# RWKV-7 chunks: Z and Y formed transposed in one product per head, and Y turned back before its norm

## The chip, the cores and the metric

One Trainium2 chip, one core. The time is the device time of one execution in microseconds (us), median of three runs. "Profile" is the hardware profiler's record of one execution.

## The reference, cut to what matters

A decoder layer for 1040 prompt rows (16 meta tokens, 1024 prompt rows) and 8 sample rows. One branch of it is RWKV-7 time mixing with 8 heads of 64 channels. Its recurrence, run over the prompt rows one by one:

```python
def step(state, inp):
    r_t, w_t, k_t, v_t, kk_t, a_t = inp
    s_kk = jnp.einsum('bhvk,bhk->bhv', state, kk_t)
    state = (state * w_t[:, :, None, :]
             - s_kk[..., None] * (kk_t * a_t)[:, :, None, :]
             + v_t[..., None] * k_t[:, :, None, :])
    return state, jnp.einsum('bhvk,bhk->bhv', state, r_t)
...
mu = jnp.mean(y, axis=-1, keepdims=True)
var = jnp.mean(jnp.square(y - mu), axis=-1, keepdims=True)
y = ((y - mu) * lax.rsqrt(var + GN_EPS)).reshape(bsz, t, D_RWKV)
y = y * lw['ln_x_w'].astype(f32) + lw['ln_x_b'].astype(f32)
out = (y + bonus.reshape(bsz, t, D_RWKV)) * g
```

The rest of the layer (forgetting attention, gates, output projection, MLP) is not touched by the change.

## The kernel before, in words

The prompt is cut into NC = 10 chunks of C = 104 rows. Each chunk replaces the loop over rows by products of 104 rows at once, for 8 heads (h), which lie as 4 pairs (p) of two halves (e) of 64 partitions. Engines run their own instruction streams and meet through counted steps: `ch_pe`, `ch_act`, `ch_dve`, `ch_pool`, with `wait(...)` on a named step. A chunk goes like this.

1. Prologue. DVE: four scans (L1891), lm (L1893), r (L1895), k (L1897), b (L1898), a (L1900), with three exponentials on ACT between them. DVE and ACT start it when PE has turned back Y of the chunk before (step "yt", `y_back`, L995).
2. PE turns K, B, V to natural layout (`natural`, L1006, 12 transposes), then forms the products of K and B with AR (L1053, 208 columns moving). DVE masks them into MK and MB (L1909).
3. Z, in natural layout (rows of the chunk on partitions): MK standing, V moving (L1062), and AR standing, the state St moving (L1065). ACT copies it to Zm.
4. DVE prepares the start of a triangular inverse (L1916, L1918, L1922) and subtracts a weight tile for the filler (L589); then six levels of halving: PE t1 (L1022, L1023), ACT copies, PE t2x, DVE subtracts (L1939). Levels 1 to 4 use these forms, 5 and 6 smaller ones (L1090, L1103, L1112).
5. u = inverse by Z (L1129); ACT negates it to NU. Y in natural layout: AR by St (L1133), MK by V (L1136), then MB by NU (L1141). Then the state's product (L1145, L1148), "s".
6. DVE: sum and mean of Y per head, state_sum and state (L1976, L1978), center, sq, var; ACT Ln and Exp; DVE norm (L1984). PE turns Y back (`y_back`), ACT scales it (L1595), POOL adds the bonus and multiplies by the gate (L2335, L2338).

Between these steps PE works on another job, the input projection of the attention branch and the gates: `fill.run(n)` issues n pieces of 3 matmuls (L384, L385, L386), 48 pieces in each chunk. Where they stand, and how many, is written by hand. Each piece is independent of the chunk's own data. The first chunk's pieces are one full-precision matmul each (L388). Between chunk 0 and 1 DVE makes eight low halves of the filler's input (L1990); the first eight pieces of chunk 1 wait for one each.

After the last chunk PE, DVE and SP start the sample rows; SP loads the samples' state dS when the chunk steps of PE and DVE are done.

Of the kernel before, what the change touches and what calls it, by code (L numbers as in the profile page):

```python
# [39 lines left out]
AX = mybir.AxisListType  # L40

P = 128
# [7 lines left out]
C = 104  # L50
NC = TP // C
HD = 64
NH = 8
# [78 lines left out]
def build(nc, A):  # L132
    with ExitStack() as ctx:
# [416 lines left out]
        NU = T1.rearrange("p a b -> p (a b)")  # L550
        Yc = Xm.rearrange("p a b -> p (a b)")
# [42 lines left out]
        LEVELS = range(1, N_LV)  # L594
# [3 lines left out]
                      + [f"{t}_{lv}_{q}" for lv in LEVELS for t in ("t1", *(("t2x",) if lv < N_LV - 1 else ()),  # L598
                                                                    *(("t2",) if lv >= N_LV - 2 else ()))
                         for q in range(2)]  # L600
                      + ["u", "y", "s", "yt"])
        ch_act = Steps(sem("ch_act"), ["v", "e1", "e3", "e2", "nat_k", "z"]
                       + [f"t1_{lv}_{q}" for lv in LEVELS for q in range(2)]
                       + ["nu", "ln", "rstd"] + [f"y_{p}" for p in range(HP)])
# [6 lines left out]
                       + ["sum", "mean", "state_sum", "state", "center", "sq", "var", "norm"])  # L611
# [41 lines left out]
        def _(sp):  # L653
# [116 lines left out]
            sp.dma_start(A["o_sp"], St).then_inc(sp_stored, 16)  # L770
            sp.dma_start(dS.rearrange("p b h k -> p (b h k)"), A["st"]).then_inc(ds_load, 16)
# [120 lines left out]
        def _(pe):  # L892
# [105 lines left out]
            def pe_chunk(c):  # L998
# [29 lines left out]
                def z_out(e, p):  # L1028
                    return PS[0:C, 2 + e, p * HD:(p + 1) * HD]
# [40 lines left out]
                for lv in LEVELS[:-1]:  # L1070
                    for q in range(2):
                        if q == 0:
                            pe.wait_ge(ch_pool.sem, ch_pool.after(c, f"bm_{lv}_low"))
                        if lv > 1:
                            wait(ch_dve, f"x_{lv - 1}_{q}_x")
                        for j in range(4):
                            last = by_halves(q, j, Bm[lv % 2], Xm, 4 * q + j)
                        ch_pe.done(last, f"t1_{lv}_{q}")
                    if IN_LEVEL[lv - 1]:
                        fill.run(IN_LEVEL[lv - 1])  # L1080
                    for q in range(2):
                        wait(ch_act, f"t1_{lv}_{q}")
                        if lv > 1:
                            wait(ch_dve, f"x_{lv - 1}_{q}_xt")
                        for j in range(4):
                            h = 4 * q + j
                            if lv < N_LV - 2:
                                last = by_halves(2 + q, j, XTr, T1, h)
                            else:
                                last = pe.matmul(PS[top, 2 + q, j * HB:(j + 1) * HB], XTr[top, h], T1[top, h],  # L1090
                                                 start=True, stop=True)
                        ch_pe.done(last, f"t2x_{lv}_{q}")
                for q in range(2):
                    for j in range(4):
                        last = by_halves(4 + q, j, T1, XTr, 4 * q + j)
                    ch_pe.done(last, f"t2_{N_LV - 2}_{q}")

                lv = N_LV - 1
                for q in range(2):
                    wait(ch_dve, f"x_{lv - 1}_{q}_x")  # L1100
                    for j in range(4):
                        h = 4 * q + j
                        last = pe.matmul(PS[low, q, j * HB:(j + 1) * HB], MB[top, h, 0, low], Xm[top, h],  # L1103
                                         start=True, stop=True)
                    ch_pe.done(last, f"t1_{lv}_{q}")
                fill.run(2)
                for q in range(2):
                    wait(ch_act, f"t1_{lv}_{q}")
                    wait(ch_dve, f"x_{lv - 1}_{q}_xl")
                    for j in range(4):  # L1110
                        h = 4 * q + j
                        last = pe.matmul(PS[top, 4 + q, j * HB:j * HB + HR], T1[low, h], XTF[low, h, low],  # L1112
                                         start=True, stop=True)
                    ch_pe.done(last, f"t2_{lv}_{q}")
# [4 lines left out]
                def y_out(e, p):  # L1119
                    return PS[0:C, 2 + e, p * HD:(p + 1) * HD]  # L1120

# [3 lines left out]
                fill.run(2)  # L1125
                wait(ch_act, "z")
                wait(ch_dve, f"x_{N_LV - 1}_1_xt")
                for h, e, p, rows in by_rows():
                    last = pe.matmul(u_out(e, p), XTF[0:C, h], Zm[0:C, h * HD:(h + 1) * HD], start=(p == 0),  # L1129
                                     stop=(p == HP - 1), skip_group_check=True)  # L1130
# [19 lines left out]
                ch_pe.done(last, "s")  # L1150
                fill.run()
# [299 lines left out]
        def _(act):  # L1451
# [77 lines left out]
            def act_chunk(c, gates, early=True):  # L1529
# [12 lines left out]
                act.wait_ge(ch_dve.sem, ch_dve.before(c))  # L1542
                act.wait_ge(st_in, 16 * c + 16)
# [13 lines left out]
                ch_act.done(act.copy(Zm[0:C].rearrange("p (e n) -> p e n", e=2), PS[0:C, 2:4, 0:HP * HD]), "z")  # L1557
# [5 lines left out]
                for lv in LEVELS:  # L1563
                    for q in range(2):
# [3 lines left out]
                        part = slice(0, C) if lv < N_LV - 1 else low  # L1568
                        ch_act.done(act.copy(quad(T1, q)[part], PS[part, q, 0:4 * HB]), f"t1_{lv}_{q}")
# [13 lines left out]

                wait(ch_dve, "var")
# [195 lines left out]
        def _(dve):  # L1780
# [99 lines left out]
            def dve_chunk(c, early=True):  # L1880
# [50 lines left out]
                for lv in LEVELS:  # L1931
# [3 lines left out]
                    if lv < N_LV - 1:  # L1935
                        part = slice(0, C) if lv < N_LV - 2 else top
                        for q in range(2):
                            wait(ch_pe, f"t2x_{lv}_{q}")
                            done(dve.tensor_tensor(quad(Xm, q)[part], quad(Xm, q)[part], PS[part, 2 + q, 0:4 * HB],  # L1939
                                                   ALU.subtract), f"x_{lv}_{q}_x")  # L1940
                    for q in range(2):
# [5 lines left out]
                        if lv < N_LV - 1:  # L1947
                            done(dve.tensor_tensor(XTF[top, four, top], XTr[top, four], moved(4 + q, top, HB),
                                                   ALU.subtract), f"x_{lv}_{q}_xt")
                            done(dve.tensor_tensor(XTF[low, four, low], XTr[low, four, 0:HR], moved(4 + q, low, HR),  # L1950
                                                   ALU.subtract), f"x_{lv}_{q}_xl")
                        else:
                            done(dve.tensor_scalar(XTF[top, four, low], moved(4 + q, top, HR), -1.0, None, ALU.mult),
# [4 lines left out]
                def heads(ap):  # L1958
                    return ap.rearrange("p (h v) -> p h v", h=NH)

                def spread(ap):
                    return ap.unsqueeze(2).to_broadcast([C, NH, HD])

                def by_head(ap):
                    return ap.rearrange("p (e a v) -> p e a v", e=2, a=HP)

                def spread4(k):
                    return gst[0:C, k].rearrange("p (e a) -> p e a", e=2).unsqueeze(3).to_broadcast([C, 2, HP, HD])

                y = PS[0:C, 2:4, 0:HP * HD].rearrange("p e (a v) -> p e a v", a=HP)  # L1970
                ych = Yc[0:C].rearrange("p (a e v) -> p e a v", a=HP, e=2)
                wait(ch_pe, "y")
                done(dve.tensor_reduce(gst[0:C, 0].rearrange("p (e a) -> p e a", e=2), y, AX.X, ALU.add), "sum")
                done(dve.tensor_scalar(gst[0:C, 0], gst[0:C, 0], 1.0 / HD, None, ALU.mult), "mean")
# [4 lines left out]
                done(dve.tensor_tensor(ych, y, spread4(0), ALU.subtract), "center")  # L1979
                done(dve.tensor_tensor(by_head(Zm[0:C]), ych, ych, ALU.mult), "sq")  # L1980
                done(dve.tensor_reduce(gst[0:C, 1].rearrange("p (e a) -> p e a", e=2), by_head(Zm[0:C]), AX.X,
                                       ALU.add), "var")
                wait(ch_act, "rstd")
                done(dve.tensor_tensor(ych, ych, spread4(3), ALU.mult), "norm")  # L1984
# [493 lines left out]
```

## Time and profile before

| | |
|---|---|
| median of 3 runs | 2047.21 us (2044.97 to 2048.68) |
| profiled execution, its time | 2051.09 us |
| profiled execution, span from first to last instruction | 2049.3 us |
| PE busy | 1964.9 us, 96% of the span |
| DVE busy | 988.7 us, 48% |
| ACT busy | 625.6 us, 31% |
| POOL busy | 201.8 us, 10% |
| mean granted TensorE clock | 0.987 |

Each line of the profile names an engine, a line of the kernel and an operation. A full-precision matmul has two records in the trace (16 records are 8 matmuls), a transpose one. The chunks run from about 228 us to 772 us of the span; chunks 1 to 9 follow each other every 53.4 us. The stretch from 496 us to 552 us, used below, holds the end of one chunk and nearly all of the next.

### The profile page before, as it was taken

The numbers are of one execution on the slowest core, as the hardware profiler recorded it, in microseconds if no ns is written. First come the engines' busy times: TensorE is split into PE (matmuls) and PEld (weight loads), VectorE is DVE, ScalarE is ACT, GpSimd is POOL, SyncE is SP. The second block draws the span as 40 slices with busy tenths as digits, with TensorE's granted clock in tenths as the row PEclk, the third lists the DMA queues.
The fourth block names the chain that finished last, engine by engine and source line by source line (L and its number), as shares of the span: only waits on it lengthen the run. The fifth ranks groups of instructions, "written<-read, shape, count | busy, mean of one in ns | idle before, by whom it ended". The sixth has DMA issues, their size and how long they took to land.

```text
span 2049.3 us, 40598 instructions
## 1 busy us (share of the span) xinstructions
PE 1964.9 (96%) x16426; PEld 1821.8 (89%) x16426; DVE 988.7 (48%) x1541; ACT 625.6 (31%) x991; POOL 201.8 (10%) x177
## 2 busy tenths in 40 slices
PE   7999999999999997998898999999999999999997
PEld 7997679999999997965667999999999999999996
DVE  6556766666666665156875644322132222213334
ACT  5114333333332322254545533321032112102213
POOL 0000212222222221221110000000000000000000
PEclk9999999999999998999999999999999999999998
DMA  4213722112232217476564621111111111111112
GB/s 174 84 39 119 262 51 55 49 47 54 60 78 70 74 56 195 150 239 199 167 234 144 232 100 43 50 41 51 42 41 51 41 51 41 45 47 42 51 42 84
DMA packets 111971, 189.45 MB, mean 92 GB/s; under 512 B 62871, under 2 KB 66231, under 8 KB 110407
## 3 DMA queue, kind: packets, MB, share of 16 engines
q1 hardware_dynamic: 109542, 179.15, 27.5%
q10 hardware_dynamic: 2304, 8.50, 1.3%
q8 instruction: 97, 1.59, 0.3%
q14 instruction: 28, 0.22, 0.0%
HBM read 149.83 MB, written 37.79 MB: 92 GB/s over the span
## 4 chain that ended last, share of the span: by engine, by line
PE 72%; issue 14%; DVE 8%; DMA 2%; ACT 2%; POOL 1%; SPq 1%; ACTq 0%; DVEq 0%; POOLq 0%
PE ps L294 44%; PE ps L384 5%; PE ps L386 4%; PE ps L385 4%; PE ps L1022 2%; PE ps L1023 1%; PE ps L1053 1%; DVE arena L1916 1%; DVE arena L1909 1%; PE ps L1210 1%; PE ps L1314 1%; PE ps L1269 1%; DMA normed<-in_kp 1%; PE ps L1136 1%; PE ps L1328 1%
## 5 line engine op out<-in xcount | busy, mean ns | idle before, releaser
L294 PE MATMUL ps<-h_high,wb_split 128*128 128x350 f32 (+1 forms) x1536 | 290.6, 324 | 0.0
L294 PE MATMUL ps<-ff_high,wb_split 128*128 128x350 f32 x1488 | 280.2, 323 | 0.0
L304 ACT CAST wb_split<-weights 128x1024 fp32r<-128x1024 f32 x88 | 92.3, 1049 | 592.7 <-PE ps L294 592.7
L294 PEld LDWEIGHTS ps<-h_high,wb_split 128*128 128x128 f32 x1536 | 254.5, 189 | 0.4
L294 PEld LDWEIGHTS ps<-ff_high,wb_split 128*128 128x128 f32 x1488 | 246.7, 189 | 0.0
L2248 DVE TENSOR_TENSOR arena<-arena,ps 128x1050 f32 (+1 forms) x39 | 48.7, 1249 | 311.1 <-PE ps L294 311.1
L294 PE MATMUL ps<-ff_low,wb_split 128*128 128x350 f32 x744 | 160.6, 324 | 0.0
L2329 POOL TENSOR_TENSOR arena<-arena,constants 64x512 f32<-64x512 f32 x100 | 121.7, 1217 | 332.0 <-DVE arena L1909 322.1
L386 PE MATMUL ps<-fill_high,w_fill_low 128*128 128x350 f32 x468 | 153.4, 328 | 0.0
L2265 DVE SCALAR_TENSOR_TENSOR squares<-ps,arena 128x1050 f32<-128x1050 f32 x32 | 40.1, 1253 | 220.1 <-PE ps L294 209.7
L294 PEld LDWEIGHTS ps<-ff_low,wb_split 128*128 128x128 f32 x744 | 127.0, 189 | 0.0
L1022 PE MATMUL ps<-arena 64*64 64x64 f32 x1600 | 113.2, 220 | 10.7 <-DVE arena L1939 5.3
L1022 PEld LDWEIGHTS ps<-arena 64*64 64x64 f32 x1600 | 101.2, 134 | 24.7 <-issue 15.0
L294 PE MATMUL ps<-h_high,w_split 128*128 128x350 f32 (+1 forms) x576 | 114.0, 329 | 2.9 <-DVE w_split L308 2.9
L1023 PE MATMUL ps<-arena 40*40 40x64 f32 x1600 | 109.8, 219 | 0.0
L308 DVE TENSOR_TENSOR wb_split<-weights,wb_split 128x1024 fp32r<-128x1024 f32 x88 | 107.3, 1219 | 2.3 <-DVE fox L2227 1.8
L385 PE MATMUL ps<-fill_low,w_fill 128*128 128x350 f32 x312 | 102.9, 330 | 0.0
L294 PEld LDWEIGHTS ps<-h_high,w_split 128*128 128x128 f32 x576 | 96.3, 189 | 5.7 <-DVE w_split L308 3.2
L1023 PEld LDWEIGHTS ps<-arena 40*40 40x40 f32 x1600 | 94.3, 112 | 0.0
L384 PE MATMUL ps<-fill_high,w_fill 128*128 128x350 f32 x234 | 82.5, 353 | 10.6 <-POOL w_fill_low L589 7.7
L386 PEld LDWEIGHTS ps<-fill_high,w_fill_low 128*128 128x128 f32 x468 | 90.4, 193 | 0.0
L2090 DVE CUSTOM_DVE_ANT_0 arena<-ps,arena 104x416 f32<-104x416 f32 (+3 forms) x152 | 68.1, 494 | 31.8 <-PE ps L1314 31.7
(348 smaller groups left out, 3682.4 us busy)
## 6 DMA issues: line engine op xcount, KB each, us to landing
weights<-in_wu SPq DMA_DIRECT2D x122, 512.0 KB, 3.5
normed<-in_vp SPq DMA_DIRECT2D x64, 260.0 KB, 4.6
normed<-in_kp SPq DMA_DIRECT2D x64, 256.0 KB, 4.9
arena<-chunk_dram SPq DMA_DIRECT2D x10, 1248.0 KB, 6.9
arena<-gate_dram SPq DMA_DIRECT2D x16, 525.0 KB, 4.0
chunk_dram<-arena SPq DMA_DIRECT2D x12, 520.0 KB, 5.1
chunk_dram<-fox SPq DMA_DIRECT2D x12, 520.0 KB, 4.6
arena<-samp_dram SPq DMA_DIRECT2D x10, 512.0 KB, 10.6
```

The lines of the kernel that those rows point to most:

```text
L294: last = pe.matmul(PS[:, 3 * s + g, 0:n], ws[s][wh][:, k * P:(k + 1) * P], tile_of(x[xh], k)[:, g * G:g * G + n], start=(k == 0 and wh + x ...
L304: act.copy(of[0][s][0], W[:, s]).then_inc(w_hi[s], 1)
L308: dve.tensor_tensor(of[0][s][1], W[:, s], of[0][s][0], ALU.subtract).then_inc(w_split[s], 1)
L384: self.pe.matmul(out, fill_w(s, k), HF[k][:, at], start=(i == 0), stop=False)
L385: self.pe.matmul(out, fill_w(s, k), HL[:, k, at], start=False, stop=False)
L386: last = self.pe.matmul(out, wl_, HF[k][:, at], start=False, stop=(i == KT - 1))
L1022: pe.matmul(PS[top, bank, at], a[top], b[top], start=True, stop=True)
L1023: return pe.matmul(PS[low, bank, at], a[low, 0:HR], b[low], start=True, stop=True)
L2090: dve.tensor_tensor_reduce(Sm[u % 3][0:C, e, lo:hi].rearrange("p b t -> p (b t)"), PS[0:C, 2 * (n % 2) + e, (lo - CUTS[c][0]) * C:(hi - CU ...
L2248: dve.tensor_tensor(dst, dst, grp(s), ALU.add).then_inc(evac[s], 1)
L2265: dve.scalar_tensor_tensor(g3(RL[s]), grp(s), 0.0, rstd1, ALU.max, ALU.mult)\
L2329: ch_pool.done(pool.tensor_tensor(Bm[lv % 2][part, :, 0:n], MB[part, :, 0, part], mask.unsqueeze(1).to_broadcast([n, NH, n]), ALU.mult), f ...
```

## The change

Z and the two parts of Y that need no u are formed in one go, transposed (channels on partitions, rows of the chunk in the free dimension): per head V stands (64 columns) and both masked halves of MK move (208 columns); then St stands and both halves of AR move (208 columns). The results stand in PSUM banks 2 and 3 until the end of the chunk, so the levels use banks 4 and 5 where they used 2 and 3, and 0 and 1 where they used 4 and 5. Z is copied by ACT, turned to natural layout by PE (4 transposes, step "zn") in level 4, and copied to Zm. For Y, NU stands and MB moves (104 columns); ACT copies Y, PE turns it (4 transposes, step "yn") behind the state's product, and DVE normalizes it from one bank. state_sum and state come before the sum of Y. Fillers are moved: 8 pieces before `y_back` and 8 behind it, where it was 4 and 12; none before u, where it was 2; 4 behind u, where it was 2. SP waits for ACT's last step too before it loads the samples' state.

```diff
                 if c:
-                    fill.run(4)
+                    fill.run(8)
                     y_back(c - 1)
-                fill.run(12 if c else 8)
+                fill.run(8)
...
                 for h, e, p, rows in by_rows():
-                    pe.matmul(z_out(e, p), MK[0:C, h, 0], Vn[0:C, vcols(h)], start=(p == 0), stop=False,
-                              skip_group_check=True)
+                    pe.matmul(zy_out(rows, p), Vn[0:C, vcols(h)], MK[0:C, h].rearrange("p x t -> p (x t)"),
+                              start=(p % 2 == 0), stop=False, skip_group_check=True)
                 for h, e, p, rows in by_rows():
-                    last = pe.matmul(z_out(e, p), AR[rows, p, 0], St[rows, p], start=False, stop=(p == HP - 1),
-                                     skip_group_check=True)
+                    last = pe.matmul(zy_out(rows, p), St[rows, p], AR[rows, p].rearrange("p a b -> p (a b)"),
+                                     start=False, stop=(p % 2 == 1), skip_group_check=True)
                 ch_pe.done(last, "z")
...
+                    if lv == ZN_LV:
+                        wait(ch_act, "z")
+                        wait(ch_dve, f"x_{lv - 1}_0_x")
+                        for p in range(HP):
+                            last = pe.transpose(PS[0:C, 4, p * P:(p + 1) * P], ZT[:, p], ident)
+                        ch_pe.done(last, "zn")
                     if IN_LEVEL[lv - 1]:
                         fill.run(IN_LEVEL[lv - 1])
                     for q in range(2):
-                        wait(ch_act, f"t1_{lv}_{q}")
+                        wait(ch_act, "zn" if lv == ZN_LV else f"t1_{lv}_{q}")
...
-                fill.run(2)
-                wait(ch_act, "z")
+                wait(ch_act, "zn")
                 wait(ch_dve, f"x_{N_LV - 1}_1_xt")
...
                 ch_pe.done(last, "u")
-                for h, e, p, rows in by_rows():
-                    pe.matmul(y_out(e, p), AR[rows, p, 1], St[rows, p], start=(p == 0), stop=False,
-                              skip_group_check=True)
-                for h, e, p, rows in by_rows():
-                    pe.matmul(y_out(e, p), MK[0:C, h, 1], Vn[0:C, vcols(h)], start=False, stop=False,
-                              skip_group_check=True)
-                fill.run(2)
+                fill.run(4)
                 wait(ch_act, "nu")
                 for h, e, p, rows in by_rows():
-                    last = pe.matmul(y_out(e, p), MB[0:C, h, 1], NU[0:C, h * HD:(h + 1) * HD], start=False,
-                                     stop=(p == HP - 1), skip_group_check=True)
+                    last = pe.matmul(zy_out(rows, p, slice(1, 2)), NU[0:C, h * HD:(h + 1) * HD], MB[0:C, h, 1],
+                                     start=False, stop=True, skip_group_check=True)
                 ch_pe.done(last, "y")
...
                 ch_pe.done(last, "s")
+                wait(ch_act, "y")
+                for p in range(HP):
+                    last = pe.transpose(PS[0:C, 0, p * P:(p + 1) * P], YS_c[:, p], ident)
+                ch_pe.done(last, "yn")
                 fill.run()
```

New on ACT, and on SP behind the last chunk:

```diff
+                ch_act.done(act.copy(ZT.rearrange("p (b a) t -> p b a t", b=2), zy_part(0)), "z")
...
+                    if lv == ZN_LV:
+                        wait(ch_pe, "zn")
+                        ch_act.done(act.copy(Zm[0:C], PS[0:C, 4, :]), "zn")
...
+                wait(ch_pe, "y")
+                ch_act.done(act.copy(YS_c.rearrange("p (b a) t -> p b a t", b=2), zy_part(1)), "y")
...
+            sp.wait_ge(ch_act.sem, ch_act.before(NC))
             sp.dma_start(dS.rearrange("p b h k -> p (b h k)"), A["st"]).then_inc(ds_load, 16)
```

## Rows read from the trace of the kernel before

**Rows 1.** The page: the chain that ended last, share of the span by engine.

```profile
PE 72%; issue 14%; DVE 8%; DMA 2%; ACT 2%; POOL 1%; SPq 1%; ACTq 0%; DVEq 0%; POOLq 0%
```

**Rows 2.** Chain of waits, 496 to 552 us: start us, us, what.

```profile
510.64 1.31 PE ps L1006 x12
511.95 1.59 PE ps L1053 x16
...
524.17 0.42 DVE arena L1939
...
543.34 0.35 PE ps L384
...
544.48 1.43 PE ps L1129 x16
545.92 0.88 PE ps L1133 x16
546.80 1.61 PE ps L1136 x16
548.40 0.21 PE ps L384
...
549.42 1.43 PE ps L1141 x16
550.85 0.62 PE ps L1145 x16
```

**Rows 3.** Timeline of PE: start, us, engine, line, form, count, [idle before <-releaser].

```profile
232.16 1.71 PE L1006 MATMUL ps<-constants,arena 128*104 128x128 f32 x12 [1.50 <-DVE arena L1897]
...
510.48 1.47 PE L1006 MATMUL ps<-constants,arena 128*104 128x128 f32 x12
...
517.36 1.59 PE L1062 MATMUL ps<-arena 104*104 104x64 f32 x16
...
522.09 0.27 PE L1022 MATMUL ps<-arena 64*64 64x64 f32 x1
```

**Rows 4.** Timeline of DVE over the norm, the next prologue and level 6.

```profile
498.55 0.42 DVE L1976 TENSOR_TENSOR arena<-arena,ps 128x256 f32<-128x256 f32 x1 [0.19 <-PE ps L1148]
...
503.49 0.69 DVE L1984 TENSOR_TENSOR arena<-arena 104x512 f32<-104x512 f32 x1 [1.89 <-ACT arena L1588]
504.98 1.60 DVE L1891 TENSOR_TENSOR_SCAN arena<-constants,arena 128x104 f32<-128x104 f32 x4 [0.79 <-PE ps L995]
506.61 1.31 DVE L1893 TENSOR_TENSOR arena<-arena 128x416 f32<-128x416 f32 x1
...
509.45 0.59 DVE L1897 TENSOR_TENSOR arena<-arena 128x416 f32<-128x416 f32 x1
...
543.37 0.32 DVE L1953 TENSOR_SCALAR arena<-ps 64x160 f32<-64x160 f32 x1
```

**Rows 5.** Timeline of DVE in chunk 0's prologue, and between chunks 0 and 1.

```profile
230.24 0.59 DVE L1893 TENSOR_TENSOR arena<-arena 128x416 f32<-128x416 f32 x1
...
281.92 7.07 DVE L1990 TENSOR_TENSOR fill_low<-normed,fill_high 128x1050 fp32r<-128x1050 f32 x6
...
291.23 3.14 DVE L1891 TENSOR_TENSOR_SCAN arena<-constants,arena 128x104 f32<-128x104 f32 x4
```

**Rows 6.** Timeline of PE in level 1: two heads' top halves behind each other.

```profile
524.05 0.22 PE L1022 MATMUL ps<-arena 64*64 64x64 f32 x1
...
524.11 0.22 PE L1022 MATMUL ps<-arena 64*64 64x64 f32 x1
```

**Rows 7.** Windows: stretch, busy us (count) of PE, PEld, DVE, ACT, POOL, PEclk, DMA, GB/s.

```profile
232.00:233.00 1.00, 0.84 (x6) 0.61 (x7) 0.93 (x3) 0.52 (x3) 0.00 (x0) 1.00 1.02 404
...
772.00:779.00 7.00, 5.40 (x24) 4.54 (x23) 0.00 (x0) 4.04 (x7) 2.12 (x2) 0.51 0.97 331
```

**Rows 8.** Timeline of ACT behind u, and behind the last chunk.

```profile
545.95 0.60 ACT L1580 ACTIVATE arena<-ps 104x512 f32<-104x512 f32 x1 [4.36 <-PE ps L1129]
...
772.35 1.43 ACT L1595 ACTIVATE arena<-ps,params 128x104 f32<-128x104 f32 x4 [1.21 <-PE ps L995]
```

More of the change, by code:

```diff
@@ L550, in build @@
         NU = T1.rearrange("p a b -> p (a b)")
+        ZT, YS_c = Lm, E3
         Yc = Xm.rearrange("p a b -> p (a b)")
@@ L592, in build @@
         bonus_added = sem("bonus_added")
-        LEVELS = range(1, N_LV)
+        LEVELS, ZN_LV = range(1, N_LV), N_LV - 3
         IN_LEVEL = (0, 0, 0, 8, 2)
@@ L597, in build @@
                       + [f"prod_{m}{i}" for i in range(2) for m in "kb"] + ["z"]
[L598 to L601, printed above, removed]
+                      + [x for lv in LEVELS for t in ("t1", *(("zn",) if lv == ZN_LV else ()),
+                                                      *(("t2x",) if lv < N_LV - 1 else ()),
+                                                      *(("t2",) if lv >= N_LV - 2 else ()))
+                         for x in ([t] if t == "zn" else [f"{t}_{lv}_{q}" for q in range(2)])]
+                      + ["u", "y", "s", "yn", "yt"])
         ch_act = Steps(sem("ch_act"), ["v", "e1", "e3", "e2", "nat_k", "z"]
-                       + [f"t1_{lv}_{q}" for lv in LEVELS for q in range(2)]
-                       + ["nu", "ln", "rstd"] + [f"y_{p}" for p in range(HP)])
+                       + [x for lv in LEVELS for x in [f"t1_{lv}_{q}" for q in range(2)] + ["zn"] * (lv == ZN_LV)]
+                       + ["nu", "y", "ln", "rstd"] + [f"y_{p}" for p in range(HP)])
         ch_dve = Steps(sem("ch_dve"), [f"scan_{p}" for p in range(HP)] + ["lm", "r", "k", "b", "a", "nat_b", "nat_v"]
@@ L610, in build @@
                                           for t in (("xt", "xl") if lv == N_LV - 2 else ("xt",))])]
-                       + ["sum", "mean", "state_sum", "state", "center", "sq", "var", "norm"])
+                       + ["state_sum", "state", "sum", "mean", "center", "sq", "var", "norm"])
         ch_pool = Steps(sem("ch_pool"), [f"bm_{lv}_{b}" for lv in LEVELS[:-1] for b in ("top", "low")] + ["bonus", "gate"])
@@ L1026, in by_rows, with zy_out @@
                     return [(h, h // HP, h % HP, hrows(h)) for p in range(HP) for h in (p, p + HP)]
-                def z_out(e, p):
-                    return PS[0:C, 2 + e, p * HD:(p + 1) * HD]
+                def zy_out(rows, p, x=slice(0, 2)):
+                    at = p % 2 * 2 * C
+                    return PS[rows, 2 + p // 2, at + x.start * C:at + x.stop * C]
                 if c:
-                    fill.run(4)
+                    fill.run(8)
                     y_back(c - 1)
-                fill.run(12 if c else 8)
+                fill.run(8)
                 wait(ch_dve, "k")
@@ L1087, in pe_chunk @@
                             if lv < N_LV - 2:
-                                last = by_halves(2 + q, j, XTr, T1, h)
+                                last = by_halves(4 + q, j, XTr, T1, h)
                             else:
-                                last = pe.matmul(PS[top, 2 + q, j * HB:(j + 1) * HB], XTr[top, h], T1[top, h],
+                                last = pe.matmul(PS[top, 4 + q, j * HB:(j + 1) * HB], XTr[top, h], T1[top, h],
                                                  start=True, stop=True)
@@ L1094, in pe_chunk @@
                     for j in range(4):
-                        last = by_halves(4 + q, j, T1, XTr, 4 * q + j)
+                        last = by_halves(q, j, T1, XTr, 4 * q + j)
                     ch_pe.done(last, f"t2_{N_LV - 2}_{q}")
@@ L1102, in pe_chunk @@
                         h = 4 * q + j
-                        last = pe.matmul(PS[low, q, j * HB:(j + 1) * HB], MB[top, h, 0, low], Xm[top, h],
+                        last = pe.matmul(PS[low, 4 + q, j * HB:(j + 1) * HB], MB[top, h, 0, low], Xm[top, h],
                                          start=True, stop=True)
@@ L1111, in pe_chunk @@
                         h = 4 * q + j
-                        last = pe.matmul(PS[top, 4 + q, j * HB:j * HB + HR], T1[low, h], XTF[low, h, low],
+                        last = pe.matmul(PS[top, q, j * HB:j * HB + HR], T1[low, h], XTF[low, h, low],
                                          start=True, stop=True)
@@ L1117, in u_out @@
                     return PS[0:C, 4 + e, p * HD:(p + 1) * HD]
[L1119 to L1120 removed]
                 def s_out(rows, p):
                     return PS[rows, 1, p * HD:(p + 1) * HD]
[L1125 to L1126 removed]
+                wait(ch_act, "zn")
                 wait(ch_dve, f"x_{N_LV - 1}_1_xt")
                 for h, e, p, rows in by_rows():
[L1129 removed]
+                    last = pe.matmul(u_out(e, p), XTF[0:C, h], Zm[0:C, vcols(h)], start=(p == 0),
                                      stop=(p == HP - 1), skip_group_check=True)
                 ch_pe.done(last, "u")
[L1132 to L1138 removed]
+                fill.run(4)
                 wait(ch_act, "nu")
                 for h, e, p, rows in by_rows():
[L1141 to L1142 removed]
+                    last = pe.matmul(zy_out(rows, p, slice(1, 2)), NU[0:C, h * HD:(h + 1) * HD], MB[0:C, h, 1],
+                                     start=False, stop=True, skip_group_check=True)
                 ch_pe.done(last, "y")
@@ L1542, in act_chunk @@
                 act.wait_ge(ch_dve.sem, ch_dve.before(c))
+                act.wait_ge(ch_act.sem, ch_act.before(c))
                 act.wait_ge(st_in, 16 * c + 16)
@@ L1556, in act_chunk, with zy_part @@
                 wait(ch_pe, "z")
-                ch_act.done(act.copy(Zm[0:C].rearrange("p (e n) -> p e n", e=2), PS[0:C, 2:4, 0:HP * HD]), "z")
+                def zy_part(x):
+                    return PS[:, 2:4, 0:4 * C].rearrange("p b (a x t) -> p b a x t", a=2, x=2)[:, :, :, x]
+                ch_act.done(act.copy(ZT.rearrange("p (b a) t -> p b a t", b=2), zy_part(0)), "z")
                 def quad(ap, q):
@@ L1567, in act_chunk @@
                             wait(ch_pe, f"{'t2x' if lv < N_LV - 1 else 't2'}_{lv - 1}_{q}")
-                        part = slice(0, C) if lv < N_LV - 1 else low
-                        ch_act.done(act.copy(quad(T1, q)[part], PS[part, q, 0:4 * HB]), f"t1_{lv}_{q}")
+                        part, bank = (slice(0, C), q) if lv < N_LV - 1 else (low, 4 + q)
+                        ch_act.done(act.copy(quad(T1, q)[part], PS[part, bank, 0:4 * HB]), f"t1_{lv}_{q}")
+                    if lv == ZN_LV:
+                        wait(ch_pe, "zn")
+                        ch_act.done(act.copy(Zm[0:C], PS[0:C, 4, :]), "zn")
                     if lv == 4:
@@ L1938, in dve_chunk @@
                             wait(ch_pe, f"t2x_{lv}_{q}")
-                            done(dve.tensor_tensor(quad(Xm, q)[part], quad(Xm, q)[part], PS[part, 2 + q, 0:4 * HB],
+                            done(dve.tensor_tensor(quad(Xm, q)[part], quad(Xm, q)[part], PS[part, 4 + q, 0:4 * HB],
                                                    ALU.subtract), f"x_{lv}_{q}_x")
@@ L1947, in dve_chunk @@
                         if lv < N_LV - 1:
-                            done(dve.tensor_tensor(XTF[top, four, top], XTr[top, four], moved(4 + q, top, HB),
+                            done(dve.tensor_tensor(XTF[top, four, top], XTr[top, four], moved(q, top, HB),
                                                    ALU.subtract), f"x_{lv}_{q}_xt")
-                            done(dve.tensor_tensor(XTF[low, four, low], XTr[low, four, 0:HR], moved(4 + q, low, HR),
+                            done(dve.tensor_tensor(XTF[low, four, low], XTr[low, four, 0:HR], moved(q, low, HR),
                                                    ALU.subtract), f"x_{lv}_{q}_xl")
                         else:
-                            done(dve.tensor_scalar(XTF[top, four, low], moved(4 + q, top, HR), -1.0, None, ALU.mult),
+                            done(dve.tensor_scalar(XTF[top, four, low], moved(q, top, HR), -1.0, None, ALU.mult),
                                  f"x_{lv}_{q}_xt")
                 fill_split_low(dve, c + 1, 0)
[L1958 to L1974, printed above, removed]
                 wait(ch_pe, "s")
@@ L1978, in dve_chunk, with heads, spread @@
                 done(dve.tensor_tensor(St, St, E1[:, :, C - 1:C].to_broadcast([P, HP, HD]), ALU.mult), "state")
[L1979 to L1982, printed above, removed]
+                def heads(ap):
+                    return ap.rearrange("p (h v) -> p h v", h=NH)
+                def spread(k):
+                    return gst[0:C, k].unsqueeze(2).to_broadcast([C, NH, HD])
+                y, ych = heads(PS[0:C, 0, :]), heads(Yc[0:C])
+                wait(ch_pe, "yn")
+                done(dve.tensor_reduce(gst[0:C, 0], y, AX.X, ALU.add), "sum")
+                done(dve.tensor_scalar(gst[0:C, 0], gst[0:C, 0], 1.0 / HD, None, ALU.mult), "mean")
+                done(dve.tensor_tensor(ych, y, spread(0), ALU.subtract), "center")
+                done(dve.tensor_tensor(heads(Zm[0:C]), ych, ych, ALU.mult), "sq")
+                done(dve.tensor_reduce(gst[0:C, 1], heads(Zm[0:C]), AX.X, ALU.add), "var")
                 wait(ch_act, "rstd")
-                done(dve.tensor_tensor(ych, ych, spread4(3), ALU.mult), "norm")
+                done(dve.tensor_tensor(ych, ych, spread(3), ALU.mult), "norm")
             dve_chunk(0, early=False)
```

## The prediction

> **What bounds the kernel now.** I read the page first: PE is busy for 96% of the span (the table above) and makes 72% of the chain that ended last [rows 1]. So I asked two things of each edit: how many microseconds PE gains or loses, and where PE has to stand still. The chain of waits over one chunk [rows 2] then shows where the chunk is PE's and where another engine's. From about 542 us to the end it is PE without a break. At 524.17 us it is DVE's subtraction L1939, which came free only when DVE was done with its masks and weight split. PE had started level 1 at 522.09 [rows 3] and was some 0.4 us ahead. The timelines [rows 3, 4] give the slack at the other meeting points. Chunks follow each other every 53.4 us, so a change per chunk counts about nine times.
>
> **The prices of the new forms.** None is in the trace exactly, but each has close neighbours. The count of records is 16 for 8 full-precision matmuls.
> - V standing (64 columns, output alternating between the partition halves), 208 columns moving. Neighbour one is L1145, the same halves with 64 moving: 0.62 us for 16 records, 39 ns each [rows 2]. Neighbour two is L1053, 208 moving: 1.59 us. L1053 against L1133 (64 moving, 0.88 us) gives 0.31 ns per record and moving column. So 39 + 144 x 0.31 = 84 ns, 1.34 us, from one side and 1.59 us from the other. I take 1.5.
> - St standing on half the rows, output in the same half, 208 moving. L1022 starts every 0.06 us with an L1023 in between [rows 6], so 30 ns a record at 64 columns; 30 + 45 = 75 ns, 1.2 us; from above L1053's 1.59. I take 1.4.
> - NU standing, 104 moving: 39 + 40 x 0.31 = 51 ns, 0.82 us; scaling L1145 wholly by columns gives 1.01. I take 0.87.
> - Four transposes: 12 take 1.47 us less overlap [rows 3], some 0.11 us each, 0.45 us, and I add 0.05 for the change of form: 0.5.
> - A filler piece of 3 records: six records took 543.34 to 544.48, the first 0.35 [rows 2], so 0.16 each and 0.48 us a piece.
>
> **One steady chunk, from one yt to the next.**
> 1. Prologue. y_back ends near 504.84. DVE then has scans, lm, r, k, and k ends at 509.45 + 0.59 = 510.04 [rows 4], 5.2 us behind yt. PE filled this with 12 pieces and came at 510.48 [rows 3], 0.44 late. With 8 pieces it comes 4 x 0.48 = 1.9 us earlier, at 508.55, and stands still until 510.1: a new stall of 1.55 us. The natural block starts 0.38 us earlier relative to yt. The four pieces are not gone; they are term 7.
> 2. Z. Before: 1.59 us less overlap for MK by V [rows 3], 1.5, and 0.9 for AR by St, whose form is that of L1133 [rows 2]; 2.4 us. After: 1.5 + 1.4 = 2.9. PE, some 0.25 us early at Z, comes to level 1 at +0.5 - 0.25 = +0.25 us, DVE up to 0.4 us earlier as its chain also started earlier. DVE was last here, with some 0.4 us to spare for PE, so the extra product is hidden behind DVE's split. Net -0.1, bounds -0.4 (DVE alone) to +0.2 (both products at 1.59).
> 3. zn in level 4: +0.5. The eight pieces behind it (3.9 us) hide ACT's copy to Zm, 0.6 us by its nearest row, L1580 [rows 8].
> 4. Before u the two pieces are gone. PE ends level 6 at 543.34, but u needs the last L1953, which ends at 543.37 + 0.32 = 543.69 [rows 4], so u starts at about 543.8 in place of 544.48: -0.7, with 0.45 us of it a new wait.
> 5. Between u and y: out go 0.88 + 1.61 + (549.42 - 548.40 = 1.02) = 3.51 us; in come 4 pieces, 0.21 + 11 x 0.16 = 1.95. Net -1.56. NU needs 0.65 us behind u [rows 8], well hidden by 1.95.
> 6. y: 1.43 becomes 0.87, -0.56.
> 7. yn +0.5, and 16 pieces between yn and y_back where 12 stood: +1.9. ACT's copy of Y (0.6 us again) has the state's product (1.1 us) over it.
>
> Sum: -0.1 + 0.5 - 0.7 - 1.56 - 0.56 + 0.5 + 1.9 = 0.0 us a chunk. Counted otherwise: PE's own work falls by 3.05 us a chunk (Y's two products and the cheaper third) and rises by 1.5 (Z and the two turns), a gain of some 1.5; the 2.0 us of new standing still in the prologue and before u, less some 0.5 us for which PE stood or came late at the same places before, take it away.
>
> The norm chain: before it ran from the end of s (498.5) to 504.18, with sum and mean in front of it. After, behind s come state_sum, state, sum, mean, center, sq, var, Ln, Exp, norm, 6.65 us. PE comes to y_back 0.5 + 7.8 us behind s, so nothing waits. POOL, SP's stores of y and the weight loads behind them move with yt and have room.
>
> **The ends.** Chunk 0 ends its own norm about 0.4 us earlier: Z +0.5, zn +0.5, u -0.8, between -1.1, y -0.56, norm chain +0.9. Then DVE makes the eight low halves (8 x 1.17 us, [rows 5]). Before, y_back(0) stood behind four of them and DVE went into its scans at once (291.23). Now it stands behind all eight and three more matmuls: 1.5 us later. Net +1.1. The last chunk has no pieces over its norm: -0.1 + 0.5 - 0.7 - 1.56 - 0.56 = -2.4, and the norm comes 0.95 us later behind y: -1.45. SP then loads the samples' state only after ACT's four L1595, 1.43 us [rows 8]; the queue was full there (DMA share 1.00, [rows 7]), so between 0 and 1.4, I take 0.4. Total: 1.1 + 8 x 0.0 - 1.45 + 0.4 = 0.0 us.
>
> Against the profiled execution that is 2051.1 us; the median of the runs stood 3.9 us below it, so 2047.2. I say 2047.5, since the prologue's stall has the larger upside. With 0.3 us a chunk unsure, times nine, and 1.5 at the ends, this case reaches from 2043.5 to 2051.5. A change under 0.2%, 4.1 us, is what a measurement of this kernel can hardly tell from none.
>
> **Rivals.**
> - The halves do not overlap at 208 columns (slower). The pairs St by AR of both row halves now write one bank, where L1065 wrote two. If that serialises them, the block takes 3.0 in place of 1.4 us; 0.4 of the 1.6 is hidden by DVE, and ten chunks pay 12 to 16 us: 2061. It decides from 0.4 us on. Against it: L1022 and L1023 write two halves of one bank and start 30 ns apart [rows 6], where each takes 220 ns. Chance 0.09. The Trainium skill, "TensorEngine Tiling (Array Packing)", Restrictions and Gotchas, Gotcha 1, says that different row tiles cannot use the same PSUM bank at once; by it the rival would be the forecast. The rows of level 1 disagree with it.
> - The clock falls in the new stall (slower). PE stands still for 1.55 us and then has 1.4 us of transposes. Behind the last chunk PE waited for the norm, did four transposes and waited for ACT's 1.43 us [rows 8], and the granted clock was 0.51 over the next 7 us, the 1.2 GHz level [rows 7]. Each fall costs the chunk up to 3 us. In chunk 0 PE stood still for 1.50 us before the same transposes [rows 3] and the clock stayed at 1.00 [rows 7]. If three of nine chunks fall: +7, 2054.5; if all: 2070. Chance 0.15. The Trainium skill, "TensorE: Matmul & The Clock Gate", "HAM oscillation — how this bites in real kernels", warns of waits that return in every iteration; the single case in chunk 0 speaks against it here.
> - The prologue is shorter and the stall does not come (faster). lm took 0.59 us in chunk 0 [rows 5] and 1.31 in a steady chunk [rows 4], where POOL works on the bonus. If POOL's work fell elsewhere, k would come 1.3 us earlier and so would every chunk: 8 x -1.3, 2037. It decides from 0.5 us on. Against it: POOL, like DVE, starts from yt in both. Chance 0.08.
> - The moved waits hurt elsewhere: in level 4 or before yn PE waits for ACT's new copies, 0.3 to 0.6 us a chunk, 2051. Chance 0.08.
>
> **The numbers.** Forecast 0.60, rivals 0.09, 0.15, 0.08, 0.08. Of the forecast's case 0.07 lies below and 0.07 above the 0.2%. Faster 0.08 + 0.07 = 0.15. Slower 0.09 + 0.15 + 0.07, less those clock falls that cost under 4 us (0.04), plus half of the last: 0.31. Same 0.54. The range takes the forecast's case, the last rival and a few clock falls: 2043 to 2058; it leaves out the faster rival, the serial banks and the worst clock.
>
> **What would show it.** Right: chunks still 53.3 to 53.6 us apart; PE idle some 1.5 us before the natural block for L1897's counterpart, some 0.4 before u; the merged product at 2.7 to 3.1 us; granted clock at 1.00 through chunks 1 to 9. Wrong: a merged product over 3.3 us, PE idle before level 1's first product or before yn, clock at 0.50 in chunks, or k earlier than 5 us behind yt.

## The result and the profile after

The changed kernel takes 2068.02 us (median of 4 runs, 2061.97 to 2069.42), against 2047.30 us before. The ratio is 1.0092, with a 95% interval of 1.0078 to 1.0107: slower by 0.9%. The range of the prediction ended at 2058.

The page of the changed kernel, its span and its engines' busy time:

```profile
span 2066.9 us, 40174 instructions
...
PE 1968.1 (95%) x16186; PEld 1806.8 (87%) x16186; DVE 987.4 (48%) x1541; ACT 636.3 (31%) x1011; POOL 197.9 (10%) x177
```

PE's busy time grew by 3.2 us although its work shrank. The span grew by 17.6 us. The first scan of each chunk (L1891 before, L1905 after) places the loss. Distances between these starts, worked out from the timelines of DVE, in us; chunk 0 begins at 228.6 and 228.4:

| chunk to chunk | 0-1 | 1-2 | 2-3 | 3-4 | 4-5 | 5-6 | 6-7 | 7-8 | 8-9 |
|---|---|---|---|---|---|---|---|---|---|
| before | 62.6 | 53.45 | 53.43 | 53.43 | 53.44 | 53.43 | 53.47 | 53.45 | 53.35 |
| after | 65.8 | 53.9 | 55.28 | 55.33 | 53.81 | 55.33 | 56.88 | 55.34 | 53.66 |

There are three lengths: 53.8, 1.5 more, and 3.0 more. The eight steady distances are 12.1 us longer in sum, the start (up to chunk 1's first scan) 2.9, the last chunk 0.7, and what comes behind the chunks 1.9, which was not followed up. The windows over chunk 5's end show what the 1.5 are (columns as in rows 7):

```profile
553.00:554.00 1.00, 1.00 (x9) 1.00 (x9) 0.26 (x1) 0.00 (x0) 0.00 (x0) 0.58 0.00 0
554.00:555.00 1.00, 1.00 (x5) 1.00 (x5) 0.00 (x0) 0.60 (x1) 0.00 (x0) 0.50 0.00 0
555.00:556.00 1.00, 1.00 (x5) 1.00 (x4) 0.00 (x0) 0.00 (x0) 0.00 (x0) 0.50 0.07 16
556.00:557.00 1.00, 1.00 (x6) 0.95 (x5) 0.00 (x0) 0.00 (x0) 0.00 (x0) 0.72 0.00 0
```

From about 553.2 us on, for some 3.4 us, the granted clock is 0.50, the 1.2 GHz level. PE's timeline over the same place says what it had done before, and what it pays:

```profile
550.44 1.12 PE L1122 MATMUL ps<-arena 40*64 40x40 f32 x16
552.06 2.03 PE L1135 MATMUL ps<-arena 104*104 104x64 f32 x16 [0.50 <-DVE arena L1967]
553.85 0.64 PE L384 MATMUL ps<-fill_high,w_fill1b 128*128 128x350 f32 x1
554.28 0.49 PE L385 MATMUL ps<-fill_low,w_fill1b 128*128 128x350 f32 x1
...
556.60 0.32 PE L384 MATMUL ps<-fill_high_b,w_fill1b 128*128 128x350 f32 x1
```

L1135 is u. PE stood still for 0.50 us before it, for DVE's last step of level 6; before the change two filler pieces lay there [rows 2]. The clock fell 1.1 us after u had begun, in the middle of it, and the filler's records started 0.29 us apart in place of 0.16. Six of chunks 1 to 9 have such a stretch (one of 6.8 us), and chunk 0. The wait of 0.50 us stands before u in all of them.

The prologue, where the prediction had put a possible fall of the clock, in the same chunk. PE first, then DVE, then the windows:

```profile
517.61 1.71 PE L1009 MATMUL ps<-constants,arena 128*104 128x128 f32 x12 [1.39 <-DVE arena L1911]
519.24 1.66 PE L1057 MATMUL ps<-arena 64*104 64x208 f32 x16
...
524.91 1.63 PE L1066 MATMUL ps<-arena 104*64 104x208 f32 x16
526.47 1.62 PE L1069 MATMUL ps<-arena 64*64 64x208 f32 x16
528.02 0.43 PE L384 MATMUL ps<-fill_high,w_fill 128*128 128x350 f32 x1
```

```profile
503.75 0.42 DVE L1973 TENSOR_TENSOR arena<-arena,ps 128x256 f32<-128x256 f32 x1 [4.26 <-PE ps L1148]
...
509.72 0.69 DVE L1991 TENSOR_TENSOR arena<-arena 104x512 f32<-104x512 f32 x1 [1.89 <-ACT arena L1602]
512.49 1.60 DVE L1905 TENSOR_TENSOR_SCAN arena<-constants,arena 128x104 f32<-128x104 f32 x4 [2.08 <-PE ps L998]
514.12 1.32 DVE L1907 TENSOR_TENSOR arena<-arena 128x416 f32<-128x416 f32 x1
...
516.96 0.59 DVE L1911 TENSOR_TENSOR arena<-arena 128x416 f32<-128x416 f32 x1
...
532.01 0.96 DVE L1953 TENSOR_TENSOR arena<-arena,ps 104x256 f32<-104x256 f32 x2 [0.40 <-PE ps L1026]
```

```profile
516.00:517.00 1.00, 0.22 (x2) 0.00 (x0) 0.88 (x2) 0.79 (x3) 0.39 (x1) 1.00 0.00 0
517.00:518.00 1.00, 0.39 (x4) 0.39 (x4) 0.97 (x2) 0.00 (x0) 0.00 (x0) 1.00 0.00 0
```

The stall before the natural block is there, 1.39 us for 1.55 forecast, and the clock stays at 1.00 through it, in all chunks of this execution. The two merged products take 1.56 and 1.55 us from start to start. And DVE now waits 0.40 us for PE in level 1, where it came last before.

### The profile page after: what moved, and what is told of

Its sections match the earlier page's. It is cut to its first block, busy times and chain, and to the rows that moved or that the text cites. A ratio compares the mean times of both kernels' runs of the same rounds, so it can differ in the third digit from the quotient of the medians.

```text
span 2066.9 us, 40174 instructions
## 1 busy us (share of the span) xinstructions
PE 1968.1 (95%) x16186; PEld 1806.8 (87%) x16186; DVE 987.4 (48%) x1541; ACT 636.3 (31%) x1011; POOL 197.9 (10%) x177
## 3 DMA queue, kind: packets, MB, share of 16 engines
q8 instruction: 95, 1.56, 0.3%
## 4 chain that ended last, share of the span: by engine, by line
PE 56%; issue 29%; POOL 6%; DMA 3%; DVE 3%; SPq 2%; ACT 1%; POOLq 0%; ACTq 0%; DVEq 0%
PE ps L294 44%; POOL arena L2336 5%; PE ps L384 2%; PE ps L385 2%; PE ps L386 2%; DMA weights<-in_wu 1%; DMA normed<-in_kp 1%; PE ps L1214 1%; SPq L816 1%; PE ps L1318 1%; PE ps L1332 1%; PE ps L1348 1%; PE ps L1273 1%; SPq L822 1%; DMA normed<-in_vp 1%
## 5 line engine op out<-in xcount | busy, mean ns | idle before, releaser
L1953 DVE TENSOR_TENSOR arena<-arena,ps 104x256 f32<-104x256 f32 (+1 forms) x100 | 42.0, 420 | 90.2 <-PE ps L1026 68.5
```

## The experiments

Theory A, formed from these lines: the clock falls because PE stands still before u, behind the small products of levels 5 and 6. Rival B: it falls from the longer wait before the natural block, or from the new products and turns. The last two columns of the table are taken from each profiled execution: the distance of chunks without a fall, and how many of chunks 1 to 9 have a stretch at half clock behind the start of u (one execution each; the other executions have no such count). Ratios are to runs of the kernel before on the same chip; medians of different rows come from different chips.

| kernel | median us | ratio to before, 95% | chunk us | falls |
|---|---|---|---|---|
| changed kernel | 2068.02 | 1.0092 (1.0078 to 1.0107) | 53.8 | 6 |
| two_before_u | 2048.62 | 0.9988 (0.9974 to 1.0001) | 53.27 | 0 |
| four_before_yback | 2049.81 | 0.9995 (0.9981 to 1.0009) | 52.5 | 5 |
| both_back | 2036.41 | 0.9931 (0.9905 to 0.9958) | 52.03 | 0 |
| old_none_before_u | 2077.17 | 1.0120 (1.0095 to 1.0146) | 53.96 | 5 |
| old_eight_eight | 2061.99 | 1.0078 (1.0056 to 1.0101) | 55.19 | 0 |
| one_before_u | 2050.73 | 1.0005 (0.9991 to 1.0020) | 53.32 | 0 |
| both_back_moved_one | 2029.24 | 0.9906 (0.9889 to 0.9922) | 51.58 | 0 |
| two_more_in_level5 | 2062.35 | 1.0062 (1.0038 to 1.0086) | 53.8 | 6 |
| moved_one_one_before_u | 2034.98 | 0.9927 (0.9900 to 0.9955) | 51.63 | 0 |

**two_before_u.** Two of the four pieces behind u go back before it.

```diff
+                fill.run(2)
                 wait(ch_act, "zn")
...
-                fill.run(4)
+                fill.run(2)
                 wait(ch_act, "nu")
```

> The changed kernel, with two of the four filler pieces behind u put back before u, as it was. Theory A (the clock falls because PE, without these pieces, stands still before u in a stretch of small products): no stretch at half clock in chunks 0 to 9 except between chunks 0 and 1; chunks 53.4 to 53.6 us apart; 2050 to 2055 us. Rival B (the falls come from the longer wait before the natural block, or from the turned Z and Y): still five to eight falls, chunks mostly 55 us apart, 2063 to 2068 us.

The ratio goes from 1.0092 to 0.9988, some 21 us. Some 4 us of that are the wait itself: 53.27 us a chunk against 53.8 without a fall. One window over chunks 1 to 8 for each shows the clock, the changed kernel first:

```profile
305.00:775.00 470.00, 447.37 (x5793) 401.11 (x5790) 284.71 (x465) 152.41 (x321) 127.11 (x106) 0.98 0.24 62
```

```profile
305.00:760.00 455.00, 437.31 (x5787) 392.39 (x5784) 282.94 (x464) 152.37 (x321) 127.06 (x106) 1.00 0.24 62
```

No fall behind u is left, at an edit that touches neither the stall before the natural block nor the new products. The chunk distance came out a little below the expectation, 53.27.

**four_before_yback.** The other moved fillers go back.

```diff
                 if c:
-                    fill.run(8)
+                    fill.run(4)
                     y_back(c - 1)
-                fill.run(8)
+                fill.run(12 if c else 8)
```

> The changed kernel, with four filler pieces before the turning back of Y and twelve behind it, as it was. Theory A: the falls stay, since the place before u is as in the changed kernel; the stall of 1.4 us before the natural block goes; chunks without a fall 52.3 to 52.7 us apart, with one 54.1; 2054 to 2058 us. Rival B, that the wait before the natural block makes the clock fall: no falls, 2042 to 2047 us.

In the profiled execution the falls stay (chunks 1, 3, 4, 8 and 9) and the stall goes: distances of 52.5 us, and 54.0 to 54.3 with a fall. Chunk 4's u has its wait, and the natural block of the next chunk has none:

```profile
491.80 1.65 PE L1135 MATMUL ps<-arena 104*104 104x64 f32 x16 [0.50 <-DVE arena L1967]
```

```profile
511.76 1.47 PE L1009 MATMUL ps<-constants,arena 128*104 128x128 f32 x12
```

The median, 2049.81, is below the expected 2054; the profiled execution was the slowest of ten (2056.29). How many falls the others had is not on record; their mean granted clocks reach from 0.979 to 0.986, with 0.980 in the profiled one, so most probably had fewer. Rival B's first half, the wait before the natural block, is out: that wait is gone and the clock still falls.

**both_back.** Both edits together.

```diff
+                fill.run(2)
                 wait(ch_act, "zn")
...
-                fill.run(4)
+                fill.run(2)
                 wait(ch_act, "nu")
...
-                    fill.run(8)
+                    fill.run(4)
                     y_back(c - 1)
-                fill.run(8)
+                fill.run(12 if c else 8)
```

> The changed kernel with both fillers' places as before: two pieces before u and two behind, four before the turning back of Y and twelve behind. Theory A: no falls and no stall, chunks 52.0 to 52.4 us apart, 2039 to 2044 us, faster than the kernel before. If the products themselves are what costs, it stays at 2050 us or above.

2036.41 us, 0.7% faster than before, with a distance of 52.03. So the change without its moves of the fillers (the transposed products, their two turns and DVE's new order) gains 1.4 us a chunk; both moves together lost more than that. Two waits are left, one at level 1 and one at y_back. Its DVE and its PE:

```profile
518.06 0.97 DVE L1954 TENSOR_TENSOR arena<-arena,ps 104x256 f32<-104x256 f32 x2 [0.32 <-PE ps L1026]
```

```profile
497.72 0.58 PE L998 MATMUL ps<-constants,arena 104*128 104x104 f32 x4 [0.39 <-DVE arena L1992]
```

**old_none_before_u.** The same cut in the kernel before, without anything else of the change.

```diff
-                fill.run(2)
                 wait(ch_act, "z")
                 wait(ch_dve, f"x_{N_LV - 1}_1_xt")
...
-                fill.run(2)
+                fill.run(4)
                 wait(ch_act, "nu")
```

> The kernel before, with one edit: the two filler pieces before u are moved behind it (none before u, four before the last part of Y). Theory A: the clock falls here too, in four to eight chunks just behind the start of u, chunks 53.7 us apart without a fall and 55.2 with one; 2055 to 2062 us. Rival B: no falls, only some 0.3 us a chunk more, 2049 to 2051 us.

The clock falls here too, so neither the new products nor the turns are needed for it. The time is far above the expectation, 2077.17 us, since a fall lasts longer, 6.8 or 10.2 us in place of 3.4: distances of 57.06 and 58.65 us beside 53.96, 3.1 and 4.7 us more. PE's timeline at one of them:

```profile
503.79 1.65 PE L1128 MATMUL ps<-arena 104*104 104x64 f32 x16 [0.50 <-DVE arena L1952]
505.37 1.01 PE L1132 MATMUL ps<-arena 64*104 64x64 f32 x16
506.32 3.03 PE L1135 MATMUL ps<-arena 104*104 104x64 f32 x16
509.11 0.64 PE L384 MATMUL ps<-fill_high,w_fill1b 128*128 128x350 f32 x1
```

The wait before u is the same 0.50 us. Behind u come more small products here, where the changed kernel has its filler at once. That this keeps the clock down longer is likely from the two timelines, but wasn't tried by itself.

**old_eight_eight.** The split of the other filler in the kernel before.

```diff
                 if c:
-                    fill.run(4)
+                    fill.run(8)
                     y_back(c - 1)
-                fill.run(12 if c else 8)
+                fill.run(8)
```

> The kernel before, with one edit: eight filler pieces before the turning back of Y and eight behind it, in place of four and twelve. If the stall before the natural block is a cost of this split alone: 1.4 to 1.5 us of PE standing still there in chunks 2 to 9, chunks 54.8 to 55.1 us apart in place of 53.4, 2060 to 2064 us, and the granted clock at 1.00 in chunks 1 to 8. If the stall makes the clock fall: chunks 56.5 us apart in some, above 2067 us.

The cost is the split's alone, 2061.99 us, and the clock stays up. A window from chunk 1 into chunk 9:

```profile
305.00:775.00 470.00, 450.10 (x5975) 414.08 (x5971) 283.26 (x465) 142.94 (x304) 128.29 (x106) 1.00 0.24 61
```

PE stands still before the natural block for 1.3 to 1.4 us in chunks 2 to 9, in L1006's view by source for PE:

```profile
its engine sat idle before it (us, times) until:
  DVE arena L1897: 12.9, 10
```

A chunk costs 55.19 - 53.43 = 1.76 us more, a little over the expected 1.5.

**one_before_u.** Is it the standing still, or how little PE does around it? One piece covers the 0.5 us.

```diff
+                fill.run(1)
                 wait(ch_act, "zn")
...
-                fill.run(4)
+                fill.run(3)
                 wait(ch_act, "nu")
```

> The changed kernel with one filler piece before u and three behind (it had none and four). One piece covers the 0.5 us for which PE stood still. If the standing still is what makes the clock fall: no falls in chunks 1 to 9, chunks 53.4 to 53.6 us apart, 2050 to 2055 us. If it is the amount of dense work in that stretch: falls in one to four chunks, 2055 to 2062 us.

No falls, 53.32 us. One piece is as good as two, within the noise (1.0005 and 0.9988, with intervals that overlap).

**two_more_in_level5.** The other side of that question: the wait before u stays, and the stretch ahead of it gets two more pieces.

```diff
-        IN_LEVEL = (0, 0, 0, 8, 2)
+        IN_LEVEL = (0, 0, 0, 6, 4)
```

> The changed kernel, still with no filler piece before u, so that PE still stands still there for 0.5 us; but two pieces are moved from level 4 into level 5 (six and four, in place of eight and two), some 5 us ahead of u. If the standing still before u by itself makes the clock fall: five to eight falls as in the changed kernel, 2063 to 2070 us. If it is how little PE does over the whole stretch from level 5 to u: fewer falls, none to two, chunks 53.8 us apart, 2053 to 2058 us.

The falls stay: distances of 55.3 to 55.5 us in four places, 56.93 in one and 53.7 to 53.8 in three, and a fall in the last chunk. Its timeline, again behind the wait of 0.50 us:

```profile
556.97 1.70 PE L1135 MATMUL ps<-arena 104*104 104x64 f32 x16 [0.50 <-DVE arena L1967]
558.43 0.64 PE L384 MATMUL ps<-fill_high,w_fill1b 128*128 128x350 f32 x1
558.87 0.49 PE L385 MATMUL ps<-fill_low,w_fill1b 128*128 128x350 f32 x1
```

More filler 5 us ahead does not help, one piece in the gap does. The piece in the gap takes away the standing still and adds work right before u at once; no run separates the two.

**both_back_moved_one.** both_back still showed DVE waiting 0.32 us for PE in level 1, and PE waiting 0.39 us for the norm. One piece is moved from the first place to the second. The edit is against both_back.

```diff
-                    fill.run(4)
+                    fill.run(5)
                     y_back(c - 1)
...
                 ch_pe.done(last, "z")
-                fill.run(4)
+                fill.run(3 if c else 4)
```

> The changed kernel with both fillers' places as before, and one further piece moved from behind Z to before the turning back of Y (three behind Z, five before y_back), where PE stood still for 0.39 us. PE no longer comes late to level 1 (DVE waited 0.32 us for it there). Theory: chunks 51.7 to 51.9 us apart in place of 52.03, 2032 to 2036 us. If DVE's wait in level 1 had another cause: 52.1 to 52.2 us apart and 2037 to 2039.

2029.24 us, 0.94% faster than before, the fastest here; the chunk distance is 51.58, 0.45 us less, somewhat more than expected. Both waits are gone from its DVE timeline and from L998's view (2.3 us in one place, the last chunk, where both_back had 5.4 in nine):

```profile
514.31 1.35 DVE L590 TENSOR_TENSOR w_fill_low<-weights,w_fill1b 128x512 fp32r<-128x512 f32 x1
515.58 0.95 DVE L1954 TENSOR_TENSOR arena<-arena,ps 104x256 f32<-104x256 f32 x2
```

**moved_one_one_before_u.** The same, against both_back_moved_one, with one piece before u and three behind.

```diff
-                fill.run(2)
+                fill.run(1)
                 wait(ch_act, "zn")
...
-                fill.run(2)
+                fill.run(3)
                 wait(ch_act, "nu")
```

> The fastest kernel so far (both fillers' places back, one piece moved from behind Z), with one piece before u and three behind it in place of two and two. One piece covers the wait of 0.5 us. Theory: as one_before_u against two_before_u, no falls in chunks 1 to 9 and the period within 0.1 us of 51.6, 2028 to 2034 us. If its margin against the falls is gone with the shorter period: some falls of 1.5 us each, 2035 to 2042 us.

No falls in chunks 1 to 9 and 51.63 us a chunk, as expected; its median of 2034.98 us has its interval overlapping that of the kernel above, so nothing is gained.

## Why the prediction was wrong

The forecast was no change, 2047.5 us; it came out 20.5 above. The step that failed is step 4. It took the removal of the two pieces before u as a gain of 0.7 us "with 0.45 us of it a new wait" and asked nothing more of that wait. The wait was there with nearly the size forecast, 0.50 us. Behind it the clock fell in 6 of chunks 1 to 9 and in chunk 0, and with the wait filled it fell in none (two_before_u, one_before_u). In the steady distances this is four times 1.5 and once 3.0 us, 9 of 12.1 us. The prediction had a rival for the clock, at 0.15, but put it at the other new stall, the one of 1.4 us before the natural block. There the clock never fell in the profiled executions, neither in the changed kernel nor in old_eight_eight. The sign that it named for being wrong, the clock at 0.50 in chunks, came, but at u.

Step by step for a steady chunk without a fall, each the distance of the same two instructions in the timelines, after minus before (steps 1 to 4 from the chunk whose scans start at 512.49, the others from the one at 458.68, against the chunk at 504.98):

| step | forecast | measured |
|---|---|---|
| 1, 2: prologue and Z, to level 1's first L1939 | -0.1 | 19.52 - 19.19 = +0.33 |
| 3: zn in level 4 | +0.5 | +0.39 |
| 4: u starts earlier | -0.7 | -0.49 |
| 5, 6: u to the end of s | -2.12 | -2.20 |
| 7: end of s to the next scan | +2.4 | +2.31 |
| sum | 0.0 | +0.34 |

- The gain of step 4 was over-counted too, 0.7 for 0.49. It took u's start, 544.48, from the chain of waits and the end of DVE's L1953 from the timeline, where u starts earlier:

```profile
544.32 1.59 PE L1129 MATMUL ps<-arena 104*104 104x64 f32 x16
```

- Step 2 was mis-sized. The merged products cost 3.1 us, not 2.9, and PE came to Z 0.04 us later behind the scans than before, not 0.25 earlier. The natural block takes 1.63 us from start to start, 0.2 more; [rows 3] had it already, 1.71 us behind a wait in chunk 0 and 1.47 in a steady chunk. From the second L1053 to Z it is another 0.2 more. PE reached level 1 late, past DVE's 0.4 us of room. Over eight distances the 0.38 us that a chunk without a fall is longer make 3 of the 12.1 us. both_back_moved_one took it back: with one piece less behind Z the wait in level 1 is gone.
- Step 1's stall was right (1.39 for 1.55), and so was its meaning: four_before_yback is 1.3 us a chunk shorter.
- The ends. Chunk 1's scans come 2.9 us later than before, for 1.1 forecast; two_before_u, which has no fall in chunk 0, has them 1.1 us later. That the two agree is no proof: the terms that the forecast lists for chunk 0 add up to -0.56, not to the -0.4 it used, and two_before_u has two filler pieces before u where the forecast had none. While DVE makes the low halves between chunks 0 and 1, the clock is at half in both kernels, for 6.8 us before and 10.2 after; what that adds was not separated. The last chunk, forecast 1.45 us shorter, is 0.7 longer and has a fall too. SP's new wait, put at 0.4 us, cost nothing that shows: the samples' state is loaded 2.15 us behind y_back where it was 1.28, but the store that follows is issued 4.59 us behind it in both. The DMA share that the forecast called 1.00 there is 0.97 in [rows 7].
- The serial-banks rival was rightly small. St by AR, both row halves into one bank, takes 1.55 us for 16 records, as L1053 with two banks did, 1.59 [rows 2]. The Trainium skill, "TensorEngine Tiling (Array Packing)", Restrictions and Gotchas, Gotcha 1, has different row tiles unable to use one bank at the same time. The rows of this form, each tile writing its own half of the partitions, disagree.
- Whether two halves overlap at 208 columns is read against a full-precision matmul on the whole array, filler pieces of chunk 0:

```profile
242.60 2.62 PE L388 MATMUL ps<-normed,weights 128*128 128x350 f32 x8
```

The next group starts 2.56 us on, so this is 0.32 us a record for 350 columns, and by columns 0.19 us for 208, an estimate. The merged products' records come every 0.10 us.
- The faster rival did not come: lm took 1.32 us, and k ended 5.1 us behind the first scan, as before. The last rival did not come either: no wait for ACT's copies shows in level 4 or before yn.

The forecast's account of PE's work was right: the products gain (1.5 us a chunk forecast, 1.4 in both_back), and the places of the fillers lose. In ratios, against the changed kernel's 1.0092: two_before_u takes back 1.0%, four_before_yback 1.0%, and both together 1.6%, which ends 0.7% below the kernel before.

The Trainium skill, "TensorE: Matmul & The Clock Gate", "HAM oscillation — how this bites in real kernels", warns that waits which return with every iteration drop the clock again and again. The waits that it describes are waits for DMA of about 3 to 5 us, longer than either here. In this trace a returning wait of 0.50 us went with falls at u, and a returning one of 1.4 us at the natural block did not.

## What to carry to other kernels

When independent work is moved out of a gap, look at what PE does on both sides of the gap, not only at its length: here 0.5 us of standing still behind small products brought falls of the clock that cost 1.5 to 4.7 us each, and 1.4 us behind dense filler cost only itself. One piece of filler that just covered the wait was enough here, and two pieces a few microseconds earlier were not. And judge the products and the placing of the filler by separate runs, since here a gain of 1.4 us a chunk was hidden under two losses.

## What the runs showed of the hardware that was not expected

- The clock fell behind a wait of 0.50 us (row 552.06 above), while waits of 1.4 us in every chunk left it at 1.00. In the changed kernel it did so in 6 of 9 chunks whose instructions and waits are the same; why not in all, the runs don't settle.
- What a fall cost follows its length: 1.5 us for 3.4 us at half clock, 3.0 or 3.1 for 6.8, 4.7 for 10.2. Where dense filler followed u it was the short one in 5 of 6 chunks (changed kernel); where more small products did, it was never shorter than 6.8 us (old_none_before_u).
- V standing with 64 columns, its output alternating between the halves of the partitions, moves 208 columns in 98 ns a record, as the row halves of L1053 do in 99: both kinds of pairs overlap about alike, since the whole array would need some 190 ns (the estimate from L388 above).
